# Opening by halves of the first weight slot, and output rows of the first heads ahead of the channel mean, in a two-block fp32 transformer kernel

## What is computed

```python
y = rmsnorm(h, norm_mix_g[l]) @ w_in[l]
q = partial_rotary(y[..., 0:D_ATT].reshape(B, S, ATT_HEADS, HEAD_DIM))      # 8 heads of 64
k = partial_rotary(y[..., D_ATT:2 * D_ATT].reshape(B, S, ATT_HEADS, HEAD_DIM))
v = y[..., 2 * D_ATT:3 * D_ATT].reshape(B, S, ATT_HEADS, HEAD_DIM)
att = dilated_sliding_attention(q, k, v).reshape(B, S, D_ATT)
c0 = 3 * D_ATT
conv = conformer_conv(y[..., c0:c0 + D_CONV], y[..., c0 + D_CONV:c0 + 2 * D_CONV],
                      conv_w[l], conv_b[l], conv_ln_g[l], conv_ln_b[l])
h = h + jnp.concatenate([att, conv], axis=-1) @ w_out[l]
```

## Time and profile before

| | |
|---|---|
| device time, 3 runs | 1367.4 us median (1367.29 to 1368.0) |
| profiled execution | 1368.27 us, span 1366.4 us, mean granted clock 0.993 |
| PE busy | 1331.3 us (97%), 7374 matmuls |
| DVE busy | 1093.3 us (80%) |
| ACT busy | 847.0 us (62%) |
| POOL busy | 105.1 us (8%) |
| chain that ended last | PE 82%, DVE 11%, ACT 5%, issue 1% |

### The profile page before, as it was taken

How to read it: one execution, slowest core, us unless ns; L and a number is a source line. 1 busy time by engine, 2 the same in 40 slices (tenths; PEclk the granted TensorE clock), 3 DMA queues, 4 the chain that set the end, 5 groups by cost and what they waited for, 6 DMA issues and landing times.

```text
span 1366.4 us, 20551 instructions
## 1 busy us (share of the span) xinstructions
PE 1331.3 (97%) x7374; PEld 1144.4 (84%) x7374; DVE 1093.3 (80%) x1671; ACT 847.0 (62%) x1255; POOL 105.1 (8%) x102
## 2 busy tenths in 40 slices
PE   7999899999999999999999999999999999999999
PEld 6896697888888988898888898887888888888887
DVE  4999666757667978666666798867999999999998
ACT  4457564444446785454444559535888888888886
POOL 0000000000002122000000012200010110110111
PEclk9999999999999999999999999999999999999999
DMA  8653343555554520355555544037999999999997
GB/s 297 213 180 99 118 143 110 185 185 185 188 188 149 169 95 1 124 176 192 187 185 185 163 146 142 1 108 265 404 357 404 381 376 405 380 374 404 382 372 288
DMA packets 149554, 304.25 MB, mean 223 GB/s; under 512 B 7248, under 2 KB 79340, under 8 KB 149356
## 3 DMA queue, kind: packets, MB, share of 16 engines
q1 hardware_dynamic: 146736, 294.76, 61.0%
q0 software_dynamic: 2192, 7.87, 2.3%
q10 hardware_dynamic: 556, 0.67, 0.2%
HBM read 295.93 MB, written 7.34 MB: 222 GB/s over the span
## 4 chain that ended last, share of the span: by engine, by line
PE 82%; DVE 11%; ACT 5%; issue 1%; DMA 0%; SPq 0%; POOL 0%; DVEq 0%; ACTq 0%
PE bank L567 19%; PE bank L569 18%; PE bank L568 18%; PE bank L625 10%; PE bank L627 5%; DVE weights_split L2188 4%; DVE arena L2406 2%; ACT weights_split L1605 1%; PE bank L1118 1%; PE bank L1109 1%; PE bank L1124 1%; PE bank L1392 1%; PE bank L1088 1%; ACT probs L1662 1%; DVE features_split L2267 1%
## 5 line engine op out<-in xcount | busy, mean ns | idle before, releaser
L1605 ACT ACTIVATE weights_split<-weights 128x1024 fp32r<-128x1024 f32 (+4 forms) x266 | 258.4, 1022 | 238.7 <-PE bank L569 152.3
L2188 DVE TENSOR_TENSOR weights_split<-weights,weights_split 128x1024 fp32r<-128x1024 f32 (+4 forms) x258 | 295.0, 1186 | 129.3 <-ACT weights_split L1605 129.1
L567 PE MATMUL bank<-weights_split,features_split 128*128 128x512 f32 (+3 forms) x560 | 215.5, 385 | 3.2 <-DVE weights_split L2188 1.7
L569 PE MATMUL bank<-weights_split,features_split 128*128 128x512 f32 (+3 forms) x560 | 211.9, 378 | 0.0
L568 PE MATMUL bank<-weights_split,features_split 128*128 128x512 f32 (+3 forms) x560 | 211.6, 378 | 0.0
L625 PE MATMUL bank<-features_split,weights_split 128*128 128x512 f32 x560 | 198.1, 398 | 0.3 <-DVE weights_split L2188 0.3
L627 PE MATMUL bank<-features_split,weights_split 128*128 128x256 f32 x560 | 157.1, 281 | 0.0
L567 PE MATMUL bank<-weights_split,hidden_split 128*128 128x512 f32 x376 | 147.7, 393 | 0.0
L569 PE MATMUL bank<-weights_split,hidden_split 128*128 128x512 f32 x376 | 146.6, 390 | 0.0
L568 PE MATMUL bank<-weights_split,hidden_split 128*128 128x512 f32 x376 | 146.5, 390 | 0.0
L625 PEld LDWEIGHTS bank<-features_split,weights_split 128*128 128x128 f32 x560 | 105.2, 188 | 26.3 <-DVE weights_split L2188 0.5
(11 more groups left out here) (423 smaller groups left out, 2533.8 us busy)
## 6 DMA issues: line engine op xcount, KB each, us to landing
weights<-in_moe_gate_dram SPq DMA_DIRECT2D x34, 1024.0 KB, 9.1
weights<-in_moe_down_dram SPq DMA_DIRECT2D x24, 1024.0 KB, 11.0
weights<-in_w_in_dram SPq DMA_DIRECT2D x20, 1024.0 KB, 5.3
weights<-in_w_up_dram SPq DMA_DIRECT2D x16, 1024.0 KB, 5.4
weights<-in_w_down_dram SPq DMA_DIRECT2D x16, 1024.0 KB, 5.0
moe_weights_in_normed<-in_moe_up_dram SPq DMA_DIRECT2D x16, 1024.0 KB, 10.1
moe_weights<-in_moe_up_dram SPq DMA_DIRECT2D x16, 1024.0 KB, 9.2
moe_weights_in_residual<-in_moe_gate_dram SPq DMA_DIRECT2D x16, 1024.0 KB, 8.7
```

Of the source, the lines that this page charges most:

```text
L567: pe.matmul(ps, lhs(0), rhs(0), start=start, stop=False, skip_group_check=shared)
L569: return pe.matmul(ps, lhs(1), rhs(0), start=False, stop=stop, skip_group_check=shared)
L1605: do(act.activation(split_flat(j)[:, 0, part], raw_flat(j)[:, part], ACT.Copy), "hi", j, b)
L2188: do(dve.tensor_tensor(split_flat(j)[:, 1, part], raw_flat(j)[:, part], split_flat(j)[:, 0, part].bitcast(F32), ALU.subtract), "lo", j)
```

## The change

Two places are edited.

**Opening.** Slot 0 gets its own function, `features_out_first`: the 32 matmuls with the high part of the weights come first, 16 for each half of the slot, and wait only for `"hi", 0, b`; then the 16 with the low part, 8 for each half, waiting for a new mark `"lo_half", 0, b`. Both column groups (`c`) of a k are done in turn in one bank. On ACT `first_square(0)` moves ahead of `turned_high`.

**End of the first attention.** In round 7 PE, behind the last `xv` matmuls, takes slot 18 and runs k = 0 (heads 0 and 1) for both token tiles; in round 8, ahead of the channel mean, k = 1 for both tiles and k = 2 for tile 0. What is left of k = 2 runs behind round 9, then the variance as before. On DVE the mean is taken off ahead of the split of heads 6 and 7.

```diff
+                def features_out_first(*name):
+                    j = nslot[0]
+                    nslot[0] += 1
+                    w = split_view(j, *shape_of(j))
+                    ps = open_bank(*name)
+                    for b in range(2):
+                        pe.wait_ge(*after("hi", j, b))
+                        for k in range(4 * b, 4 * b + 4):
+                            for c in range(2):
+                                part, at = slice(c * P, (c + 1) * P), slice(c * S, (c + 1) * S)
+                                pe.matmul(ps[:, at], w[:, 0, k, part], HT[:, 0, k, :], start=(k == 0 and c == 0),
+                                          stop=False, skip_group_check=True)
+                                pe.matmul(ps[:, at], w[:, 0, k, part], HT[:, 1, k, :], start=False,
+                                          stop=False, skip_group_check=True)
+                    for b in range(2):
+                        pe.wait_ge(*after("lo_half", j, b))
+                        for k in range(4 * b, 4 * b + 4):
+                            for c in range(2):
+                                mm = pe.matmul(ps[:, c * S:(c + 1) * S], w[:, 1, k, c * P:(c + 1) * P], HT[:, 0, k, :],
+                                               start=False, stop=(k == KD_ - 1), skip_group_check=True)
+                    mm.then_inc(*cpe.mark("filled", *name))
+                    cpe.also("slot", j)
...
                 def cross_values(s):
                     if s == 8:
+                        j, w = first_rows[0]
+                        mixed_rows(0, w, (1,), (0, 1))
+                        pe.wait_ge(*after("read", "att_o", 2))
+                        mixed_rows(0, w, (2,), (0,))
                         mean_over_channels("cmean", "conv", C)
...
+                    if s == 7:
+                        first_rows.append(weights("wout"))
+                        pe.wait_ge(*after("scores_read", AH - 2))
+                        pe.wait_ge(*after("pt_copied", AH - 2))
+                        pe.wait_ge(*after("read", "att_o", 1))
+                        mixed_rows(0, first_rows[0][1], (0,), (0, 1), first=True)
...
-                pe.wait_ge(*after("scores_read", AH - 1))
-                pe.wait_ge(*after("pt_copied", AH - 1))
-                j, w = weights("wout")
-                pe.wait_ge(*after("read", "att_o", 2))
-                mixed_rows(0, w, (0, 1, 2), (0, 1), first=True)
+                j, w = first_rows[0]
+                mixed_rows(0, w, (2,), (1,))
                 mean_over_channels("cvar", "csq", SIG)
                 pe.wait_ge(*after("read", "att_o", 3))
                 mixed_rows(0, w, (3,), (0, 1)).then_inc(*cpe.mark("slot", j))
+                pe.wait_ge(*after("scores_read", AH - 1))
+                pe.wait_ge(*after("pt_copied", AH - 1))
                 j, w = weights("wout")
...
+                first_square(0)
                 act.wait_ge(*after("read", "first_gain"))
                 turned_high(0, 0, KD_)
...
-                first_square(0)
                 high(1)
                 first_square(1)
...
+                    if s > AH:
+                        conv_mean()
                     if s >= 3 and s % 2:
                         outs1(s - 2)
                     if s <= AH:
                         conv_taps(2 if s % 2 else 3 if s < AH else 2 * TAPS)
                     else:
-                        conv_mean()
                         low(1)
```

More of the change, by code:

```diff
@@ L755, in _ @@
                 for b in range(2):
-                    features_out("g", HT, "g", b)
-                    if b == 0:
+                    if b == 1:
+                        features_out("g", HT, "g", b)
+                    else:
+                        features_out_first("g", 0)
                         pe.wait_ge(*after("rstd", 0))
@@ L795, in _, with mixed_rows @@
                 cross_slot = {}
+                for c in range(2):
+                    for t in range(TT):
+                        bank_of[("wout", c, t)] = banks[2 * t + c]
+                def mixed_rows(c, w, ks, ts, first=False, last=False):
+                    for t in ts:
+                        for k in ks:
+                            mm = matmul3(bank_of[("wout", c, t)][:, :], lambda z: CAT[:, z, k, t * P:(t + 1) * P],
+                                         lambda z: w[:, z, k % 4, :], first and k == ks[0], last and k == ks[-1])
+                    return mm
+                first_rows = []
                 def cross_values(s):
                     if s == 8:
+                        j, w = first_rows[0]
+                        mixed_rows(0, w, (1,), (0, 1))
+                        pe.wait_ge(*after("read", "att_o", 2))
+                        mixed_rows(0, w, (2,), (0,))
                         mean_over_channels("cmean", "conv", C)
@@ L1711, in _ @@
                 vector_rows(1, rows_in)
-                act.wait_ge(*after("read", "first_gain"))
-                turned_high(0, 0, KD_)
                 act.wait_ge(x_in, 32)
@@ L1719, in _ @@
                 first_square(0)
+                act.wait_ge(*after("read", "first_gain"))
+                turned_high(0, 0, KD_)
                 high(1)
```

1 line of the change is left out of this document (added).

## The result

| | before | after |
|---|---|---|
| device time, median (lowest to highest, runs) | 1367.35 us (1364.39 to 1368.0, 4) | 1357.76 us (1357.35 to 1358.59, 4) |
| ratio, 95% interval | 1 | 0.9928 (0.9916 to 0.994) |
| profiled execution, span | 1368.27, 1366.4 us | 1357.95, 1356.1 us |
| mean granted clock of that execution | 0.993 | 0.999 |

The account below looks back on a forecast made before the run. PE bounds the kernel (busy 1331.3 of 1366.4 us), leaving about 35 us idle plus low-clock time. Gains 4.99 + 5.57 = 10.56 off 1368.27 give 1357.7; the median's 0.87 less, rounded, 1357.0, range 1354.0 to 1361.0.

Parts of the forecast that it names:

- Opening, start of slot 0: PE starts slot 0 at 12.27 instead of 15.70 us, once its first half is high: 3.43 us.
- the term: Opening: slot 0 ends at 18.03 instead of 23.02, 4.99 us earlier (3.43 earlier start, 1.56 clock), carried whole to the attention.
- the first rival: Opening: the clock stays low for part of slot 0 though the idle time is gone; price 1.56, time 1358.4, chance 0.12.
- the prediction's sentence that the trace doesn't agree: Opening: the skill's low-by-default clock rule is contradicted by a granted clock of 1.00 right behind PE's first idle time.
- Inside slot 0: Opening: no further wait within slot 0, all 48 matmuls at 0.12, 5.76 instead of 7.32 us.
- Attention: predicted 5.57: End of the first attention: slot 20 starts at 158.26 instead of 163.83, 5.57 us earlier.
- The prediction's lower bound for this place: Attention's end: least gain 2.7 us, idle filled but clock as before (5.57 less 1.89 and 0.9).
- Elsewhere: predicted nothing: Outside the two edited places no row should differ but in its start.
- the rival on the phase: Later stages, shifted by 10 us, may or may not meet clock falls, 1.56 each; time 1355 to 1359, chance 0.07.
- an opening not carried: Slots or small vectors arrive late and take back the opening's gain; price up to 4.99, time up to 1362, chance 0.06.
- nothing measurable: Both edited places are followed by a wait that takes all back; time 1367, chance 0.03.
- of slower: Attention, round 7: six matmuls wait for slot 18's low half and hold head 7's transposes; time 1370, chance 0.02.

Follow-up runs that it names:

- e1: Opening's edits alone (slot 0 by halves, first square sum moved) on the kernel before; 1361.51 us, ratio 0.9962.
- e3: The changed kernel without the four dummy matmuls ahead of slot 0, whose results nobody reads; 1358.81 us, ratio 0.9943 to before.
- e9: The kernel before, ten dummy matmuls instead of four in the opening and nine unread ones ahead of the channel mean; 1361.61 us, ratio 0.9962.
- e5: The kernel before with slot 0 taken by halves, first square sum not moved; 1361.74 us, ratio 0.997.
- e4: The kernel before with nine matmuls nobody reads put ahead of the channel mean; 1364.30 us, ratio 0.9979.
- e7: The kernel before with only DVE's order changed (mean taken off ahead of the split of heads 6 and 7); 1366.23 us, ratio 1.0.
- e8: The kernel before with only PE's order at the attention's end changed, DVE's untouched; 1363.90 us, ratio 0.9983.
- e2: The attention's edits alone (PE's rows and DVE's order) on the kernel before; 1361.20 us, ratio 0.9962.

## Why the prediction was right, and where it was not

**Opening, start of slot 0: predicted 12.27, in the profile 13.09.** 0.23 us are the table's later landing (6.76 instead of 6.53), the rest the dummies. The step that failed is the one that counted only slot 0's data; the dummies were taken to be out of the way, as in before, where they ended at 12.1 (10.18 + 1.89). To the root e1 takes 11.54 us, with dummies of 1.89 us, after 12.26, with dummies of 3.01, and e3 11.66, without them. So the term is 4.99 where the dummies take 1.89 us (measured 4.95), and 0.6 to 0.7 less where they take 3.01; together with the landing it was 4.00 in the profile.

**The reading of the clock in the opening was wrong.** I took the earlier trace rows, a granted clock of 1.00 at 7 to 8 us, as a measurement against the first rival. The same column stands at 1.00 from 10 to 13 us in after, over L777 with its 3.01 us, and in before (1.89 us), for the same eight matmuls; 3.78 is what eight of this shape take at the lower level. Over eleven kernels the four dummies took 1.89 or 1.90 us in three, 2.28 to 3.01 in six (none in e3), and in e9 the ten took 4.48, 0.22 us a record as in before. The transposes of x settle it: in before and after they start 0.21 to 0.22 us apart (six in the one microsecond of the earlier trace rows; only the first gap is longer), and so they do in e1, but for the last two, which follow after 0.12 and 0.10 us. So the clock was low in that very row. The first record of the clock in each trace is a rise to full, at 9.26 us in e1, 12.69 in after and 10.16 in before: in e1 the spacing of the transposes halves there, in after that of the dummies (0.43 to 0.22 us a record), and in before the dummies start there. So the column, ahead of its first recorded change, says nothing, and the durations of the matmuls do. The Trainium skill, "TensorE: Matmul & The Clock Gate", "Part 1: The HAM clock gate", says that the low clock is the default and work lifts it, and that the number of slow matmuls at a start varies from run to run; by the durations this kernel agrees (the rise came 2.9 us behind PE's first instruction in e1 and 5.9 in after, with the same instructions on PE), and the prediction's sentence that the trace doesn't agree is wrong. The rival itself came true only in the dummies, at 0.6 us and not 1.56: slot 0 ran at 0.12 a matmul in after, e1, e3 and e5, the first one apart.

**Inside slot 0**: right. No wait for the second half or the low parts, 48 matmuls in 19.02 - 13.09 = 5.93 us (5.82 in e3). The order of k and c in one bank costs nothing. Nothing behind it is late, and up to 110 us PE waits for a weight once, 0.2 us, as in the earlier trace rows.

**Attention: predicted 5.57, measured 9.33 - 4.00 = 5.33.** The variance is 4.40 us behind the mean (4.28 predicted, with 1.89 us for the mean, which took 1.99) with a wait of 0.49 (0.7), DVE is ready for it as foretold with nothing to spare (146.88, low part of slot 19 until 146.76), and the chain behind the variance took 154.50 - 146.88 = 7.62 us, as before. Slot 20 waits 0.81, not 0.5, since the next matmuls start 146.50 - 144.85 = 1.65 us behind the variance's first and not 1.89; this costs nothing. The 5.33 are 2.7 of clock (e4, e9) and 2.6 of idle time, for which rows and swap are both needed (e7, e8). The prediction's lower bound for this place, 5.57 less 1.89 and 0.9, is 2.78 and not 2.7.

**Elsewhere: predicted nothing, measured 1.0 more** in the profiled pair, 10.32 - 9.33: two falls of the clock that before met are missing, one new one came. That is the rival on the phase, which has happened besides the forecast. These falls come and go: the one at 942 us of before stands in six of the nine experiments as well (932 to 940 us), but not in after, e2, e4 and e9, and the one at 835 us in after alone. The 0.99 gained elsewhere made up for the 0.99 missing in the opening, so the median of 1357.76 beside 1357.0 owes something to two errors of opposite sign.

**The median** has the same in it. Runs of before with a mean clock of 0.997 took 1364.1 to 1365.1 us, those with 0.993 1368.3 to 1369.9; the one run of after at 0.997 took 1358.59. At equal clock the change is worth about 6 us, which is the idle part, 3.5 + 2.6; the other 3.6 us are then the clock. By the medians e1 and e2 give 5.9 and 6.2 us, together more than the 9.6 of the change. It may be that each alone raises the clock, which has 1.00 as its limit, as e1 did at the attention's end; but by the ratios they are 5.2 us each, 10.4 beside 9.8, with intervals of about 2 us to either side, so no excess is shown.

The rivals of an opening not carried, of nothing measurable and of slower have nothing for them. What stays open is what decides whether a gap meets a fall.

## What to carry to other kernels

An idle time of PE of one to four microseconds can cost more than itself, since slower matmuls may follow it; price both, and test the second by filling the gap with matmuls that nobody reads, before reordering anything. When work is moved into a gap, look at where the idle time reappears: here PE's rows alone pushed it ahead of the variance and DVE's swap alone moved nothing, and only both together shortened the chain. At a kernel's start judge the clock by what known matmuls take, and don't let warm-up matmuls end later than the first real data: here they brought nothing that the runs show (e3).

## What the runs showed of the hardware

- A similar gap meets a fall of the clock in one execution and not in the next: behind 3.62 us of idle time in before the 48 matmuls of slot 0 took 7.32 us, behind 3.28 us in e2 5.83, behind 2.81 us in e4 22.55 - 15.40 = 7.15.
- A fall at 835 us in after stands behind a wait of only 1.19 us (ahead of it PE was busy from 822 to 832 us); it lasts about three microseconds and cost 1.6 us (the shift goes from 10.1 to 8.5 us there).
- Ahead of the trace's first record of the clock the profile gives it as 1.00; the transposes of x ran at 0.21 to 0.22 us apiece there and at 0.10 to 0.12 behind the rise (e1).
- One and the same kernel varies by 0.4% (1364.1 to 1369.9 us) in step with its mean granted clock (0.997 to 0.993).
